# Modulation weights laid out over four column quarters, and 64-row score matmuls in the late attention

## The chip, the cores and the metric

The kernel runs on one core of a Trainium2 chip. The core has TensorE (matmuls, PE in the profile; its weight loads are the rows PEld), VectorE (DVE), ScalarE (ACT), GpSimd (POOL) and SyncE (SP, which here only issues DMAs). The metric is the device time of one launch in microseconds, lower is better. The kernel before takes 2261.13 us, the median of three runs (2259.18 to 2261.45).

## The reference, cut to what matters

Two transformer blocks over 256 tokens of width 2048, all in float32: the first with NSA attention, a feed-forward layer of 8192 and a gated embedding, the second (below) with a modulation computed from a vector `c`, a sliding-window attention (SWA), a latent attention (MLA) and another feed-forward layer.

```python
c_act = jax.nn.silu(c)                       # 1 x 2048
mod = c_act @ w_mod[l] + b_mod[l]            # w_mod: 2048 x 12288, 100.7 MB
sh1, sc1, g1, sh2, sc2, g2 = jnp.split(mod, 6, axis=-1)
h = rmsnorm(x, attn_norm_g[l]) * (1.0 + sc1) + sh1
proj = h @ w_in[l]
...
# SWA: 16 heads of width 64 over two key heads, keys of two blocks of 128
s = einsum('bnqhgd,bnkhd->bnhgqk', qb, k_band) * (64 ** -0.5) + bias, masked, with sinks
# MLA: 8 heads, scores are the sum of a 128-wide and a 64-wide (rotary) product
s = (einsum('bqhd,bkhd->bhqk', qn_i, k_nope) + einsum('bqhd,bkd->bhqk', qr_i, k_rope)) * scale
...
x = x + g1 * (mix @ w_out[l])
u = relu((rmsnorm(x, mlp_norm_g[l]) * (1.0 + sc2) + sh2) @ w_ff1[l])
x = x + g2 * ((u * u) @ w_ff2[l])
```

## The kernel before, in words

**The large products.** Each weight matrix comes in units of 1 MB (`raw`, four slots). A unit makes two steps. For each step ACT copies the rounded upper part (`split`, L498), DVE subtracts it from the raw value to get the lower part (`split`, L913), and TensorE multiplies both with the split activations `xs` or `hidden`. A group is eight steps and 512 output columns. In the form `columns` (L1528, L1533) a step is 16 matmuls, in the form `tokens` (L1517 to L1519) it is 12. `upper` and `lower` have four slots too: ACT may run at most four steps ahead of TensorE, and DVE follows ACT.

**The modulation.** `mod` belongs to the second block but does not depend on it, so its weights are read during the first. A mod unit is 128 rows of `w_mod` by the 2048 columns of one of six sections: one DMA of 1 MB into `modraw` (two slots), row r in partition r. `add_mod` (L917 to L930) multiplies the 128 rows by 128 values of silu(c), one for each partition, and adds to `modacc`, 128 x 2048, one DVE instruction a unit (L927; the first unit of a section is a plain multiplication, L925). After 16 units `sum_mod` (L1587) transposes `modacc` in 16 blocks of 128 x 128 on TensorE (L1592), and `store_mod` (L932) sums over the former partitions with two DVE reductions (L940) and adds the bias (L943). There are 96 mod units, two to a group, placed by hand: `group` of DVE calls `add_mod` behind the steps 3 and 6, SP issues the units behind the third and the fourth weight unit of a group (`group`, L320), and TensorE makes the sums of a section between two steps of a later group. In the stage of the gated embedding (`gated`, `regained`) DVE has the residual, two sums of squares and a gain to do for each group as well.

**The start.** Eleven small vectors are read as rows of 128 values into `vrow`, turned by three transposes (L1600) and copied to `vcol` (L1094, L1095). ACT and DVE form silu(c) as `silu_c`, 128 x 16: column k has the values for mod unit k.

**Late attention.** `LATE_JOBS` are four SWA jobs and two MLA jobs of four heads each. A job's scores (`score`, L1689) have a part for the first 128 queries (t=0, keys 128 wide) and one for the second (t=1, keys 256 wide). The head width of SWA and the rotary width of MLA are 64, but the matmuls run over 128 rows: a pair of heads stands in the two halves of `qa` or `qr`, and `ka` and `kr` are padded with zeros in the half of the other head. SWA adds the bias with matmuls from `toes` (L1715) behind the product of each head; MLA adds its 64-wide product behind the 128-wide one of each head. For t=1 heads 0 and 1 write one PSUM bank and heads 2 and 3 the next. DVE takes the maxima (L1230), ACT the exponentials (L707), DVE scales (L1257), TensorE transposes (L1736 to L1738) and multiplies with the values (`mix`, L1765 and L1766). In the SWA `mix` two heads write partitions 0 to 63 and 64 to 127 of one bank, with weights of 128 rows x 64 columns.

What sets the order is written out by hand for each engine; all waits are on semaphores that count.

Of the kernel before, what the change touches and what calls it, by code (L numbers as in the profile page):

```python
# [25 lines left out]
P = 128  # L26
# [26 lines left out]
MODS = 6 * KC  # L53

# [30 lines left out]
def program(nc, a):  # L85
    with ExitStack() as ctx:
# [36 lines left out]
        modacc = place("modacc", [P, D], at=M + 16384)  # L123
# [15 lines left out]
        vrow = place("vrow", [P, 3, P], at=U + 32768)  # L139
# [30 lines left out]
        vcol = place("vcol", [P, 2 * P + CMP_LEN])  # L170
        modcol = place("modcol", [P, 6, KC])
        modsum = place("modsum", [P, 2, KC // 2])
        silu_c = place("silu_c", [P, KC])
# [11 lines left out]
        COL = dict(mix=0, ffn=16, ple=32, attn=48, mlp=64, c=80, q=96, kv=99, b=P, k=P + 96, v=2 * P)  # L185
# [24 lines left out]
        rows_landed, aux_landed, consts = sem("rows_landed"), sem("aux_landed"), sem("consts")  # L210
# [73 lines left out]

        block = ctx.enter_context(nc.Block())
# [3 lines left out]
        def _(sp):  # L289
# [41 lines left out]
            for t in range(T):  # L331
                sp.dma_start(h[:, t, :], a["x"][0, t * P:(t + 1) * P, :]).then_inc(x_landed[t], 16)
            vecs = [(a["norm_mix"][0], 0, 0), (a["norm_ffn"][0], 16, 0), (a["norm_ple"][0], 32, 0),
                    (a["attn_norm_g_2"][0], 48, 0), (a["mlp_norm_g_2"][0], 64, 0), (a["c_2"][0], 80, 0),
                    (a["mla_q_norm_g_2"][0], 96, 0), (a["mla_kv_norm_g_2"][0], 99, 0),
# [5 lines left out]
            sp.dma_start(vrow[0:32, 2, :], a["nsa_cmp_pos_v"][0]).then_inc(rows_landed, 16)  # L341

# [3 lines left out]
            with loop(sp, c, 5, {lower_ready: 8, mod_added: 2}) as i:  # L346
                group(w_in, i * NW + 2 * NW, mods=section_rows(i * 2 + 4, 0))
# [16 lines left out]
            with loop(sp, c, NG - 1, {lower_ready: 8, mod_added: 2}) as i:  # L364
                group(w_out, i * NW + NW, mods=section_rows(i * 2 + 2, 1))
# [14 lines left out]
            with loop(sp, c, QUARTERS - 1, {lower_ready: 64, mod_added: 16}) as i:  # L380
# [3 lines left out]
            with loop(sp, c, NG, {lower_ready: 8, mod_added: 2}) as i:  # L384
# [23 lines left out]
        def _(pool):  # L408
# [32 lines left out]
            nc.gpsimd.memset(table[:], NEG).then_inc(bias_placed, 1)  # L441
            pool.wait_ge(bias_table, 1)
# [34 lines left out]
        def _(act):  # L477
# [164 lines left out]
            nc.scalar.activation(silu_c[:], vcol[:, COL["c"]:COL["c"] + KC], ACT.Sigmoid).then_inc(c_sigmoid, 1)  # L642
# [52 lines left out]
            def job_exps(n, kind, scale):  # L695
                for t in range(T):
# [4 lines left out]
                    for j in range(HPG):  # L701
                        w = P * (t + 1)
                        sb = banks_of(kind)[0]
                        src = ps[:, sb, P * j:P * j + P] if t == 0 else ps[:, sb + 1 + j // 2, S * (j % 2):S * (j % 2) + S]
# [192 lines left out]
        def _(dve):  # L897
# [19 lines left out]
            def add_mod(k):  # L917

                slot = st["mod"] % 2
                dve.wait_ge(mod_landed[slot], c.next(mod_landed[slot], 16))  # L920
                if st["mod"]:
                    dve.wait_ge(mod_added, c.at(mod_added))
                w, s = modraw[:, slot, :], silu_c[:, bass.ds(k, 1)]
                if isinstance(k, int) and k == 0:
                    op = nc.vector.tensor_scalar(modacc[:], w, s, None, ALU.mult)  # L925
                else:
                    op = nc.vector.scalar_tensor_tensor(modacc[:], w, s, modacc[:], ALU.mult, ALU.add)  # L927
                op.then_inc(mod_added, 1)
                c.next(mod_added)
                st["mod"] += 1  # L930

            def store_mod(m):  # L932
# [9 lines left out]
                link(op)  # L942
# [1073 lines left out]
```

## Time and profile before

| | |
|---|---|
| median of three runs | 2261.13 us |
| profiled execution, its own time | 2260.09 us |
| span of its instructions | 2258.2 us |
| granted TensorE clock over the span | 0.993 |
| PE busy | 2197.9 us (97%) |
| DVE busy | 1510.6 us (67%) |
| ACT busy | 1014.5 us (45%) |
| DMA | 499.5 MB, mean 221 GB/s |

The profile is of one execution; times inside it are counted from the first instruction. Busy time of PE is matmul time with modelled ends, so the starts of matmuls and weight loads say more than their lengths. A duration like 2347 ns of a DVE instruction is that instruction alone. In a timeline, neighbouring instructions of one kind are merged: `x8` is eight of them, from the start of the first to the end of the last, and square brackets tell how long the engine had been idle and what ended it. A float32 matmul that is not of the split kind is two passes in the profile, so a score product of one head is two rows x2. A transpose is one.

### The profile page before, as it was taken

What the parts mean: (1) busy time and instruction counts of PE and PEld (TensorE: products, weight loads), DVE (VectorE), ACT (ScalarE), POOL (GpSimd) and SP (SyncE); (2) the same over time, 40 slices, a digit from 0 to 9 for tenths busy, and PEclk for the clock granted to TensorE, in tenths of its full rate; (3) what the DMA queues carried; (4) which work ended last, traced back from release to release, by engine and by line L of the source; (5) the groups of instructions that cost most, each with busy time, mean ns of one, the idle gap of its engine ahead of it and who ended that gap; (6) DMA issues with size and microseconds to landing.
All of it is one profiled execution on the core that took longest, in us unless ns stands there. A gap on an engine that the chain in (4) does not pass through costs nothing.

```text
span 2258.2 us, 29043 instructions
## 1 busy us (share of the span) xinstructions
PE 2197.9 (97%) x11458; PEld 1879.8 (83%) x11458; DVE 1510.6 (67%) x1455; ACT 1014.5 (45%) x1263; POOL 15.2 (1%) x40
## 2 busy tenths in 40 slices
PE   7999999999999999999999899999999999999997
PEld 6888888788888888888878698887888888888886
DVE  6676566778677778777778866557655555555655
ACT  5443373544344344344354645545434444443442
POOL 1000000000000000000000000000000000000000
PEclk9999999999999999999999999999999999999999
DMA  8876407687877877877867463364566655655563
GB/s 313 302 265 196 154 19 298 240 281 277 300 259 288 294 277 257 318 271 284 294 237 278 125 199 118 134 202 149 185 195 193 192 187 186 198 188 192 186 198 118
DMA packets 213096, 499.50 MB, mean 221 GB/s; under 512 B 10068, under 2 KB 12680, under 8 KB 199800
## 3 DMA queue, kind: packets, MB, share of 16 engines
q1 hardware_dynamic: 211528, 491.16, 63.3%
q0 software_dynamic: 1456, 6.72, 0.8%
q8 instruction: 86, 1.41, 0.3%
q14 instruction: 26, 0.21, 0.0%
HBM read 495.68 MB, written 2.17 MB: 220 GB/s over the span
## 4 chain that ended last, share of the span: by engine, by line
PE 60%; issue 36%; DVE 2%; ACT 1%; DMA 1%; SPq 0%; POOL 0%; DVEq 0%; ACTq 0%; POOLq 0%
PE ps L1528 17%; PE ps L1517 9%; PE ps L1518 9%; PE ps L1519 9%; PE ps L1533 9%; PE ps L1709 2%; PE ps L1765 1%; PE ps L1628 1%; PE ps L1575 1%; PE ps L1592 0%; PE ps L1715 0%; ACT prob L707 0%; PE ps L1766 0%; PE ps L1763 0%; DMA raw<-in_nsa_w_in_dram 0%
## 5 line engine op out<-in xcount | busy, mean ns | idle before, releaser
L913 DVE TENSOR_TENSOR lower<-raw,upper 128x1024 fp32r<-128x1024 f32 (+2 forms) x733 | 883.9, 1216 | 517.1 <-ACT upper L498 513.7
L498 ACT ACTIVATE upper<-raw 128x1024 fp32r<-128x1024 f32 (+2 forms) x733 | 770.1, 1056 | 943.7 <-PE ps L1519 530.2
L1528 PE MATMUL ps<-xs,upper 128*128 128x512 f32 x2688 | 677.0, 394 | 0.6 <-DVE xs L1068 0.4
L1528 PEld LDWEIGHTS ps<-xs,upper 128*128 128x128 f32 x2688 | 485.8, 190 | 88.8 <-DVE xs L1068 0.8
L1517 PE MATMUL ps<-upper,hidden 128*128 128x512 f32 x1024 | 399.2, 390 | 0.0
L1518 PE MATMUL ps<-lower,hidden 128*128 128x512 f32 x1024 | 398.5, 389 | 0.0
L1519 PE MATMUL ps<-upper,hidden 128*128 128x512 f32 x1024 | 398.4, 389 | 0.0
L1533 PEld LDWEIGHTS ps<-xs,lower 128*128 128x128 f32 x2688 | 366.7, 190 | 26.2
L1533 PE MATMUL ps<-xs,lower 128*128 128x256 f32 x2688 | 374.8, 282 | 0.0
L1517 PEld LDWEIGHTS ps<-upper,hidden 128*128 128x128 f32 x1024 | 192.3, 188 | 40.3 <-DVE lower L913 0.9
L1519 PEld LDWEIGHTS ps<-upper,hidden 128*128 128x128 f32 x1024 | 192.3, 188 | 39.8
L1518 PEld LDWEIGHTS ps<-lower,hidden 128*128 128x128 f32 x1024 | 192.3, 188 | 39.5
L927 DVE SCALAR_TENSOR_TENSOR modacc<-modraw,silu_c,modacc 128x2048 f32<-128x2048 f32 x90 | 211.2, 2347 | 0.3
L1517 PE MATMUL ps<-upper,xs 128*128 128x512 f32 (+1 forms) x512 | 199.5, 390 | 3.1 <-DVE lower L913 1.9
L1519 PE MATMUL ps<-upper,xs 128*128 128x512 f32 (+1 forms) x512 | 196.9, 385 | 0.0
L1518 PE MATMUL ps<-lower,xs 128*128 128x512 f32 (+1 forms) x512 | 196.8, 384 | 0.0
L1517 PEld LDWEIGHTS ps<-upper,xs 128*128 128x128 f32 x512 | 96.3, 188 | 24.5 <-issue 4.1
L1519 PEld LDWEIGHTS ps<-upper,xs 128*128 128x128 f32 x512 | 96.1, 188 | 19.1
L1518 PEld LDWEIGHTS ps<-lower,xs 128*128 128x128 f32 x512 | 96.3, 188 | 17.8
L525 ACT ACTIVATE half<-ps 128x1024 f32<-128x1024 f32 x41 | 42.2, 1028 | 75.9 <-PE ps L1533 75.9
L980 DVE TENSOR_TENSOR summed<-ps,half 128x1024 f32<-128x1024 f32 x32 | 39.2, 1225 | 50.5 <-ACT half L525 50.5
L538 ACT ACTIVATE hidden<-summed 128x1024 fp32r<-128x1024 f32 x32 | 34.1, 1064 | 51.3 <-DVE summed L982 51.3
(259 smaller groups left out, 1160.1 us busy)
## 6 DMA issues: line engine op xcount, KB each, us to landing
raw<-in_ffn_w_dram SPq DMA_DIRECT2D x128, 1024.0 KB, 5.4
raw<-in_w_ff_dram SPq DMA_DIRECT2D x128, 1024.0 KB, 5.1
modraw<-in_w_mod_dram SPq DMA_DIRECT2D x96, 1024.0 KB, 7.3
raw<-in_nsa_w_in_dram SPq DMA_DIRECT2D x40, 1024.0 KB, 5.2
raw<-in_nsa_w_out_dram SPq DMA_DIRECT2D x16, 1024.0 KB, 7.3
raw<-in_ple_w_gate_dram SPq DMA_DIRECT2D x16, 1024.0 KB, 5.4
raw<-in_w_out_dram SPq DMA_DIRECT2D x16, 1024.0 KB, 5.0
raw<-in_w_in_dram SPq DMA_DIRECT2D x12, 1024.0 KB, 5.3
```

Of the source, the lines that this page charges most:

```text
L498: nc.scalar.activation(dst, src, ACT.Copy).then_inc(upper_ready, 1)
L525: nc.scalar.activation(half[:], ps[:, 4 * parity:4 * parity + 4, S:2 * S], ACT.Copy).then_inc(half_copied, 1)
L538: nc.scalar.activation(hidden[:, 4 * g:4 * g + 4, 0, :], summed[:], ACT.Copy).then_inc(hidden_upper, 1)
L913: nc.vector.tensor_tensor(low, src, up, ALU.subtract).then_inc(lower_ready, 1)
L927: op = nc.vector.scalar_tensor_tensor(modacc[:], w, s, modacc[:], ALU.mult, ALU.add)
L980: done(nc.vector.tensor_tensor(summed[:], ps[:, 4 * parity:4 * parity + 4, 0:S], half[:], ALU.add))
L1517: mm(out, xu, up[:, kk, :], start=first, stop=False)
L1518: mm(out, xu, low[:, kk, :], start=False, stop=False)
L1519: op = mm(out, xl, up[:, kk, :], start=False, stop=last)
L1528: mm(ps[:, 4 * par + f, :], up[:, kk, f * P:(f + 1) * P], both, start=(k == 0), stop=False, skip_group_check=True)
L1533: op = mm(ps[:, 4 * par + f, 0:S], low[:, kk, f * P:(f + 1) * P], x[:, k, 0, :], start=False, stop=(k == KC - 1), skip_group_check=True)
L1709: op = mm(out, q, k, start=first, stop=False, skip_group_check=True)
```

## The change

**Layout.** A mod unit is still 128 rows by 2048 columns, but partition 4b+q now holds rows b, 32+b, 64+b and 96+b, of each only the 512 columns of quarter q. It comes in four DMAs of 256 KB (`PARTS = 4`), runs of 2 KB instead of 8 KB. `modacc` is 128 x 512. A unit is added in four DVE instructions of 128 x 512, one for each m (rows 32m to 32m+31), each waiting for the one before it. After 16 units only four transposes are left, all into bank 2, and one DVE reduction of 128 x 512 with a stride of four sums over the 32 partitions of each quarter. `silu_c` becomes 128 x 64: each value of c four times side by side, which GpSimd writes as a copy with repetition (L457 of the new kernel) before a fourth transpose at the start.

**Scores.** For t=1 of the late jobs the 64-wide products run over 64 rows only, heads alternating between rows 0 to 63 and 64 to 127, and neighbouring heads write different banks (`late_place`). The products of the four heads now come first, and the bias matmuls, or MLA's 64-wide products, behind all four. For t=0 this order changes too, while the rows stay 128.

```diff
         modraw = place("modraw", [P, 2, D], at=M)
-        modacc = place("modacc", [P, D], at=M + 16384)
+        modacc = place("modacc", [P, D // PARTS], at=M + 16384)
...
+        def late_place(kind, j):
+            return (1 + j // 2, j % 2) if kind == "nsa" else (1 + j % 2, j // 2)
...
                 if st["mod"] >= 2:
-                    sp.wait_ge(mod_added, c.next(mod_added))
+                    sp.wait_ge(mod_added, c.next(mod_added, PARTS))
                 st["mod"] += 1
-                sp.dma_start(modraw[:, slot, :], w_mod[row, col]).then_inc(mod_landed[slot], 16)
+                src = w_mod[row, col].rearrange("(m b) (q n) -> b q m n", b=ROWS, q=PARTS)
+                for m in range(PARTS):
+                    sp.dma_start(modraw[:, slot, m * NW:(m + 1) * NW], src[:, :, m, :]).then_inc(mod_landed[slot], 16)
...
+            sp.dma_start(vrow[0:PARTS * KC, 3, 0:ROWS], a["c_2"][0].rearrange("(m b) -> m b", b=ROWS)).then_inc(rows_landed, 16)
...
+            pool.wait_ge(rows_landed, 16 * 11)
+            nc.gpsimd.tensor_copy(vrow[0:PARTS * KC, 4, :].rearrange("m (b q) -> m b q", q=PARTS),
+                                  vrow[0:PARTS * KC, 3, 0:ROWS].unsqueeze(2).to_broadcast([PARTS * KC, ROWS, PARTS])).then_inc(c_spread, 1)
...
-                dve.wait_ge(mod_landed[slot], c.next(mod_landed[slot], 16))
-                if st["mod"]:
-                    dve.wait_ge(mod_added, c.at(mod_added))
-                w, s = modraw[:, slot, :], silu_c[:, bass.ds(k, 1)]
-                if isinstance(k, int) and k == 0:
...
+                dve.wait_ge(mod_landed[slot], c.next(mod_landed[slot], 16 * PARTS))
+                for m in range(PARTS):
+                    if st["mod"] or m:
+                        dve.wait_ge(mod_added, c.at(mod_added))
+                    w, s = modraw[:, slot, m * NW:(m + 1) * NW], silu_c[:, bass.ds(k * PARTS + m, 1)]
+                    if isinstance(k, int) and k == 0 and m == 0:
+                        op = nc.vector.tensor_scalar(modacc[:], w, s, None, ALU.mult)
+                    else:
+                        op = nc.vector.scalar_tensor_tensor(modacc[:], w, s, modacc[:], ALU.mult, ALU.add)
...
-                for i, bank in enumerate((2, 6)):
-                    op = nc.vector.tensor_reduce(modsum[:, i], ps[:, bank:bank + 2, :].rearrange("p b (k n) -> p (b k) n", n=P),
-                                                 AX.X, ALU.add)
+                link(nc.vector.tensor_reduce(modsum[:].rearrange("p (i q) -> p i q", q=PARTS),
+                                             ps[:, 2, :].rearrange("p (i b q) -> p i q b", b=ROWS, q=PARTS), AX.X, ALU.add))
...
-                for k in range(KC):
-                    op = nc.tensor.transpose(ps[:, (2, 3, 6, 7)[k // 4], k % 4 * P:(k % 4 + 1) * P],
-                                             modacc[:, k * P:(k + 1) * P], ident[:])
+                for i in range(PARTS):
+                    op = nc.tensor.transpose(ps[:, 2, i * P:(i + 1) * P], modacc[:, i * P:(i + 1) * P], ident[:])
...
+                    for j in range(HPG):
+                        out = outs[j]
+                        first = j == 0 if t == 0 else late_place(kind, j)[1] == 0
                         hh = HPG * i + j
+                        r = slice(0, P) if t == 0 else slice(64 * (hh % 2), 64 * (hh % 2) + 64)
...
                         elif kind == "swa":
-                            pairs = [(qa[:, hh // 2, t * P:(t + 1) * P], ka[:, i // 2, hh % 2, 0:w])]
+                            op = mm(out, qa[r, hh // 2, t * P:(t + 1) * P], ka[r, i // 2, hh % 2, 0:w], start=first, stop=False,
+                                    skip_group_check=True)
...
+                        if kind == "mla":
+                            op = mm(outs[j], qr[r, hh // 2, t * P:(t + 1) * P], kr[r, hh % 2, 0:w], start=False, stop=False,
+                                    skip_group_check=True)
```

DVE in the second group of the gated embedding, in program order, before: `h<-h,gainrow` is the gain, `modacc` the two mod units, `lower` the splits of the weights.

```order
L1352 TENSOR_TENSOR h<-h,gainrow 128x2x512
L1340 ISA xn,sumsq_114<-h 128x512
L1340 ISA sumsq_114 128x1
L927 SCALAR_TENSOR_TENSOR modacc<-modraw,silu_c,modacc 128x2048
L913 TENSOR_TENSOR lower<-raw,upper 128x1024 x3
L927 SCALAR_TENSOR_TENSOR modacc<-modraw,silu_c,modacc 128x2048
L913 TENSOR_TENSOR lower<-raw,upper 128x1024 x4
```

The same place of the changed kernel, with what each instruction waits for:

```order
L1360 ISA xn,sumsq_114<-h 128x512 [waits gained]
L1360 ISA sumsq_114 128x1
L946 SCALAR_TENSOR_TENSOR modacc<-modraw,silu_c,modacc 128x512 [waits mod_added,mod_landed0,squares_v]
L946 SCALAR_TENSOR_TENSOR modacc<-modraw,silu_c,modacc 128x512 [waits mod_added] x3
L931 TENSOR_TENSOR lower<-raw,upper 128x1024 [waits upper_ready] x3
L946 SCALAR_TENSOR_TENSOR modacc<-modraw,silu_c,modacc 128x512 [waits mod_added,mod_landed1]
L946 SCALAR_TENSOR_TENSOR modacc<-modraw,silu_c,modacc 128x512 [waits mod_added] x3
L931 TENSOR_TENSOR lower<-raw,upper 128x1024 [waits upper_ready] x4
```

Nothing has changed its place; each unit has become four chained instructions.

TensorE in the first late job (SWA), t=0 and then t=1, before: `ka,qa` are the products, `flip,toes` the bias.

```order
L1709 MATMUL ps<-ka,qa 128x128
L1715 MATMUL ps<-flip,toes 128x128
L1709 MATMUL ps<-ka,qa 128x256
L1715 MATMUL ps<-flip,toes 128x128 x2
L1709 MATMUL ps<-ka,qa 128x256
L1715 MATMUL ps<-flip,toes 128x128 x2
```

The whole job in the changed kernel:

```order
L1732 MATMUL ps<-ka,qa 128x128 x4
L1746 MATMUL ps<-flip,toes 128x128 x4
L1732 MATMUL ps<-ka,qa 128x256 x4
L1746 MATMUL ps<-flip,toes 128x128 x8
L1994 MATMUL ps<-ident,qrope 128x128 x8
```

The four products of a part now follow one another, and the bias of all four heads comes behind them. The number of matmuls is the same.

## Rows read from the trace of the kernel before

**Rows 1.** The page, busy time of the engines.

```profile
PE 2197.9 (97%) x11458; PEld 1879.8 (83%) x11458; DVE 1510.6 (67%) x1455; ACT 1014.5 (45%) x1263; POOL 15.2 (1%) x40
```

**Rows 2.** Stretches: busy of PE, PEld, DVE, ACT, POOL; clock, DMA share, GB/s.

```profile
500.00:600.00 100.00, 100.00 (x491) 84.66 (x490) 74.08 (x57) 41.84 (x40) 0.00 (x0) 1.00 0.81 293
1200.00:1300.00 100.00, 89.83 (x404) 73.59 (x403) 82.93 (x96) 54.66 (x75) 0.00 (x0) 0.95 0.57 194
1800.00:1900.00 100.00, 100.00 (x462) 83.56 (x461) 58.20 (x48) 40.25 (x39) 0.00 (x0) 1.00 0.58 190
```

**Rows 3.** Waits of weight loads: us, times, longest.

```profile
PEld ps L1517 <- DVE lower L913: 2.2, 6, 0.4
```

**Rows 4.** Weight loads around the third section sum, first feed-forward.

```profile
712.35 1.90 PEld L1592 LDWEIGHTS ps<-ident,modacc 128*128 128x128 f32 x16
714.22 0.19 PEld L1517 LDWEIGHTS ps<-upper,hidden 128*128 128x128 f32 x1
719.83 0.19 PEld L1517 LDWEIGHTS ps<-upper,hidden 128*128 128x128 f32 x1 [0.28 <-DVE lower L913]
```

**Rows 5.** DVE around the same section sum.

```profile
712.06 1.23 DVE L989 TENSOR_TENSOR hidden<-summed,hidden 128x1024 fp32r<-128x1024 f32 x1
714.52 2.36 DVE L940 TENSOR_REDUCE modsum<-ps 128x8 f32<-128x1024 f32 x2 [1.24 <-PE ps L1592]
717.36 1.29 DVE L925 TENSOR_SCALAR modacc<-modraw,silu_c 128x2048 f32<-128x2048 f32 x1
718.56 3.49 DVE L913 TENSOR_TENSOR lower<-raw,upper 128x1024 fp32r<-128x1024 f32 x3
```

**Rows 6.** Groups of DVE: shape, count | us, mean ns | idle before.

```profile
L927 DVE SCALAR_TENSOR_TENSOR modacc<-modraw,silu_c,modacc 128x2048 f32<-128x2048 f32 x90 | 211.2, 2347 | 0.3
L1083 DVE SCALAR_TENSOR_TENSOR h<-h,norm,gainrow 128x1024 f32<-128x1024 f32 x4 | 4.9, 1279 | 1.1 <-DMA gainrow<-in_final_norm_g_dram 1.1
L1047 DVE TENSOR_SCALAR xn<-h,norm 128x512 f32<-128x512 f32 x20 | 8.4, 484 | 0.2
L982 DVE SCALAR_TENSOR_TENSOR summed<-summed 128x1024 f32<-128x1024 f32 x32 | 39.2, 1225 | 1.1
```

**Rows 7.** DVE in the second gated group, and the PEld row there.

```profile
1201.98 2.35 DVE L927 SCALAR_TENSOR_TENSOR modacc<-modraw,silu_c,modacc 128x2048 f32<-128x2048 f32 x1
1204.25 3.49 DVE L913 TENSOR_TENSOR lower<-raw,upper 128x1024 fp32r<-128x1024 f32 x3
1205.52 0.19 PEld L1517 LDWEIGHTS ps<-upper,xs 128*128 128x128 f32 x1 [0.45 <-DVE lower L913]
```

**Rows 8.** DVE and PE in a first feed-forward group, and at the start.

```profile
648.43 3.49 DVE L913 TENSOR_TENSOR lower<-raw,upper 128x1024 fp32r<-128x1024 f32 x3
651.24 1.09 PE L1528 MATMUL ps<-xs,upper 128*128 128x512 f32 x4
...
41.09 3.54 DVE L913 TENSOR_TENSOR lower<-raw,upper 128x1024 fp32r<-128x1024 f32 x3
44.84 1.32 PE L1528 MATMUL ps<-xs,upper 128*128 128x512 f32 x5
```

**Rows 9.** Fourth late job, t=1: a head's product, its bias; DVE's maximum.

```profile
1407.41 0.60 PE L1709 MATMUL ps<-ka,qa 128*128 128x256 f32 x2
1407.85 0.61 PE L1715 MATMUL ps<-flip,toes 128*128 128x128 f32 x4
...
1411.13 1.22 DVE L1230 TENSOR_REDUCE stat<-ps 128x4 f32<-128x1024 f32 x1 [0.58 <-PE ps L1715]
```

**Rows 10.** Weight loads around an SWA product with the values, 64-column weights.

```profile
1412.02 0.14 PEld L1738 LDWEIGHTS ps<-ident,prob 128*128 128x128 f32 x1
1412.33 0.20 PEld L1765 LDWEIGHTS ps<-probT,tok 128*64 128x64 f32 x4 [0.17 <-issue]
1412.60 0.36 PEld L1766 LDWEIGHTS ps<-probT,tok 128*64 128x64 f32 x4
1413.83 0.30 PEld L1709 LDWEIGHTS ps<-kn,qn 128*128 128x128 f32 x2 [0.17 <-issue]
```

More of the change, by code:

```diff
@@ L53 @@
 MODS = 6 * KC
+PARTS = 4
+ROWS = P // PARTS
 class Counts:
@@ L640, in _ @@
             to_features(vcol[:, COL["mix"]:COL["mix"] + KC], ahead=2)
-            nc.scalar.activation(silu_c[:], vcol[:, COL["c"]:COL["c"] + KC], ACT.Sigmoid).then_inc(c_sigmoid, 1)
+            nc.scalar.activation(silu_c[:], vcol[:, COL["c"]:COL["c"] + PARTS * KC], ACT.Sigmoid).then_inc(c_sigmoid, 1)
             group([first_half])
@@ L1696, in score @@
                         pe.wait_ge(exps, 2 * n - 1 + t)
+                    outs = []
                     for j in range(HPG):
-                        out = ps[:, sb, P * j:P * j + P] if t == 0 else ps[:, sb + 1 + j // 2, S * (j % 2):S * (j % 2) + S]
-                        first = j == 0 if t == 0 else j % 2 == 0
+                        bank, half_ = late_place(kind, j)
+                        outs.append(ps[:, sb, P * j:P * j + P] if t == 0 else ps[:, sb + bank, S * half_:S * half_ + S])
@@ L1700, in score @@
+                    for j in range(HPG):
+                        out = outs[j]
+                        first = j == 0 if t == 0 else late_place(kind, j)[1] == 0
                         hh = HPG * i + j
+                        r = slice(0, P) if t == 0 else slice(64 * (hh % 2), 64 * (hh % 2) + 64)
                         if kind == "nsa":
-                            pairs = [(heads[:, hh, t * P:(t + 1) * P], heads[:, 24 + 4 * b + i, 0:w])]
+                            op = mm(out, heads[:, hh, t * P:(t + 1) * P], heads[:, 24 + 4 * b + i, 0:w], start=first, stop=False,
+                                    skip_group_check=True)
@@ L1703, in score @@
                         elif kind == "swa":
-                            pairs = [(qa[:, hh // 2, t * P:(t + 1) * P], ka[:, i // 2, hh % 2, 0:w])]
-                        else:
-                            pairs = [(qn[:, hh, t * P:(t + 1) * P], kn[:, hh, 0:w]),
-                                     (qr[:, hh // 2, t * P:(t + 1) * P], kr[:, hh % 2, 0:w])]
-                        for q, k in pairs:
-                            op = mm(out, q, k, start=first, stop=False, skip_group_check=True)
-                            first = False
+                            op = mm(out, qa[r, hh // 2, t * P:(t + 1) * P], ka[r, i // 2, hh % 2, 0:w], start=first, stop=False,
+                                    skip_group_check=True)
+                        else:
+                            op = mm(out, qn[:, hh, t * P:(t + 1) * P], kn[:, hh, 0:w], start=first, stop=False,
+                                    skip_group_check=True)
@@ L1711, in score @@
+                    for j in range(HPG):
+                        hh = HPG * i + j
+                        r = slice(0, P) if t == 0 else slice(64 * (hh % 2), 64 * (hh % 2) + 64)
+                        if kind == "mla":
+                            op = mm(outs[j], qr[r, hh // 2, t * P:(t + 1) * P], kr[r, hh % 2, 0:w], start=False, stop=False,
+                                    skip_group_check=True)
                         if kind == "swa":
@@ L1880, in _ @@
             group_turned(tokens, 3)
-            group(tokens, xs, n=320, between={1: lambda: sum_mod(6 * KC), 4: turn_modulation})
+            group(tokens, xs, n=320, between={1: lambda: sum_mod(6 * PARTS * KC), 4: turn_modulation})
             group(columns, xs, between={4: turn_latents})
```

74 lines of the change are left out of this document (41 added, 33 removed).

## The prediction

> **What bounds the kernel now.** I read first the busy time of the engines [rows 1]: TensorE is busy for 97% of the span, DVE for 67%. A share is a mean, so next the stretches [rows 2]: in the first feed-forward, where modulation units are read and added, TensorE is busy for 100.00 of 100 us, DVE for 74, and the DMA engines for 0.81. In the second feed-forward, without those units, TensorE is again at 100.00. Only the stretch 1200 to 1300 has holes (PE 89.83), and there DVE is busy for 82.93. Then the waits [rows 3]: weight loads of the token groups waited for DVE's `lower` six times, 2.2 us in all. So the kernel is TensorE's almost everywhere: what is taken from its queue comes off the time one to one, what DVE gets in addition costs nothing while it stays within its lead, and the lead is gone at those six places.
>
> **The change, part by part.** The sum is made against the profiled execution, 2260.09 us (span 2258.2 and 1.9 around it); the median of the runs, 2261.13, is 1.0 above it.
>
> *Section sums, removed from TensorE.* Sixteen transposes last from 712.35 to the next group's load at 714.22, 1.87 us or 0.117 each [rows 4]. Four remain. Twelve fewer are 1.40 us, and six sections make 8.4 us. Is what follows then late? In the feed-forward DVE is at the sum at 713.29 (712.06 + 1.23) and waits 1.24 us for the transposes [rows 5]; with the transposes 1.40 earlier it starts at 713.3, 1.2 earlier. Its two reductions of 2.36 us become one of half a bank pair's width: `TENSOR_REDUCE` of 128x1024 takes 1.22 [rows 9], less 512 elements at 0.534 (the step between 1279 and 2347 ns for 1024 elements, halved [rows 6]) gives 0.69, so 1.67 us less. Behind it stands the first unit of the next section, which now has one plain multiplication and three multiply-adds. The distance to the next split was 1.20 (717.36 to 718.56) [rows 5] and becomes 0.48 for the first [rows 6] and 0.745 for each of the three (1279 ns for 128x1024 less 534 [rows 6]), with gaps of 0.03 between them (1.1 us over 32 at L982, which waits for its own predecessor [rows 6]), less the overlap of 0.08 with the next: 2.73, so 1.53 more. Net the split comes 1.2 + 1.67 - 1.53 = 1.34 us earlier, and TensorE wants it 1.40 earlier. The stall of 0.28 that stands there [rows 4] stays as it is within 0.1. I count nothing for it, and the whole 8.4 for the transposes.
>
> *The additions, lengthened on DVE.* A unit took 2.27 us of DVE's time (1201.98 to 1204.25) [rows 7]. Four of 0.745 with three gaps of 0.03, less the same 0.08, are 2.99, so 0.72 more. The elements are the same; it is three more fixed parts of about 0.21 and three waits on the own result. The trace has no multiply-add of this form at 128x512, so both ends: with the fixed part of L982 (1225 ns for 1024 elements, less 1068, is 0.16 [rows 6]) it is 0.47, and if each wait cost 0.25 more than I think it is 1.5. I take 0.72, the nearest form. Where does it show?
> - In the gated embedding the first of three splits behind the unit ends at 1204.25 + 1.22 = 1205.47, and TensorE, idle for it, starts at 1205.52 [rows 7]. No lead is left, so the 0.72 goes straight into TensorE. DVE's chain there begins anew with each group's residual, so it is paid in each of the three groups whose first unit stands behind `regained`: 2.2 us (1.4 to 4.5).
> - In the first feed-forward the corresponding split ends at 649.65 and TensorE needs it at 651.24 [rows 8]: 1.6 us of lead, 0.9 left. There are twelve such groups. Nothing, but this cover is thin: beyond a growth of 1.5 each of them would pay.
> - At the start two units stand one behind the other, 1.53 + 0.72 = 2.25 later. The split behind them ends at 41.09 + 1.22 = 42.31, and TensorE needs it at 44.84 [rows 8]: 2.5 of lead, so 0.25 left. Nothing, up to 0.3.
>
> *Four DMAs for one.* On SP's queue 288 more issues. A unit's four stand in front of the next weight unit, but SP spends most of its time waiting for free slots, and a weight unit has three others ahead of it. The DMA engines: two of six megabytes a group change from runs of 8 KB to 2 KB. The weights have runs of 2 KB already, and where only they move, 190 GB/s takes a share of 0.58, that is 328 GB/s if full [rows 2]. At that rate the 293 GB/s of the modulated stretch would take 0.89 instead of 0.81. Under 1, so nothing. The start also gets a copy on GpSimd and a fourth transpose in front of `vcol`; DVE reaches that point only after scaling its tile, and TensorE then waits for a weight unit's split on ACT. Nothing, up to 0.3 us.
>
> *Late scores.* For t=1 a head's product is two passes of 256 columns: the bias starts 0.44 us after the product (1407.41, 1407.85) [rows 9]. So the four products of a job take eight passes, 1.74 us. In pairs over different rows two passes would run side by side. Row pairs do not occur in this trace, but column pairs do: the SWA product with the values issues four loads in 0.20 us and its 256-wide passes get to the next form 0.27 us after the first (1412.33, 1412.60) [rows 10], although in program order the two forms alternate by head. So passes of two heads do overlap there. At that rate four pairs take 0.87, and 0.87 is saved. MLA's 64-wide products are the same. What goes against it are the borders of the stretch: the last full-width load before the column pairs starts at 1412.02, the next would be due at 1412.13 at the pace of transposes and starts at 1412.33, and the first behind them has 0.17 of idle again [rows 10]. I take 0.15 for each border, 0.30 a job. Net 0.57, six jobs (four SWA, two MLA): 3.4 us. Ends: 5.2 gained without borders, 1.8 lost if pairs do not overlap. Can the gain be used? DVE's maximum over t=1 waited 0.58 us for these matmuls [rows 9], so in SWA just the 0.57 goes through, and more would not.
>
> The page TensorEngine Tiling of the Trainium skill says under Key Properties that changing the tiling mode drains the engine, while different tiles may load and multiply in parallel. This speaks against short tiled stretches like these. The idle 0.17 us at both borders agrees with it; by the second half of the rule alone the late scores would give 5.2, by both 3.4.
>
> **Sum.** -8.4 + 2.2 - 3.4 = -9.6: 2250.5 against the profiled execution, and 1.0 more, 2251.5 us, against the median.
>
> **Rivals.**
> - *Row pairs don't run side by side.* Then the scores only gain two borders a job: -8.4 + 2.2 + 1.8 = -4.4, 2256.7 us. For it: no row of this trace shows two row halves at once, and both write all 128 partitions, of different banks. Against it: column pairs overlap [rows 10]. Chance 0.10.
> - *The chained additions cost more,* 1.5 us a unit. The gated embedding loses 4.5 instead of 2.2, the start 1.3 (1.53 + 0.78 + 1.5 = 3.8 against 2.5 of lead), the twelve feed-forward groups nearly nothing: -8.4 + 4.5 + 1.3 - 3.4 = -6.0, 2255.1 us. For it: a wait on the own result in front of every instruction, and indices from registers in the loops. Against it: such waits cost 0.03 at L982. Chance 0.08.
> - *The DMA engines become the bound, slower than before.* Weights take 195 of the 293 GB/s, a share of 0.595 at 328 GB/s, so the modulation's 98 GB/s took 0.215, at 456 GB/s. The place is the modulated stretch, some 1000 us; it decides once the share passes 1, with the modulation at 98 / 0.405 = 242 GB/s, and the kernel is slower than before below about 236, where 1% of 1000 us eats the gain. At 230 GB/s the share is 1.02 and the time 2251.5 + 21 = 2272. For it: four small DMAs, each with its own completion, of which the trace has no stream. Against it: the weights' 328 GB/s with the same runs. Chance 0.04.
>
> The page DMA: Bandwidth & Descriptors of the Trainium skill, under its measured HBM to SBUF table, advises batches of 1 MiB or more; 256 KB would stand far below that. It is the last rival's mechanism. No run so far shows 256 KB DMAs in a row, so it is not excluded.
>
> **How the numbers follow.** The forecast has 0.78. Its own range is 2249 to 2254. The lower end of what the bounds allow is -8.4 + 1.4 - 5.2 = -12.2, 2248.9; towards the other side the second and first rivals end at 2255.1 and 2256.7. The range 2248.5 to 2257 leaves out the DMA rival and the tails. A change of 0.2%, 4.5 us, is about what a measurement of this kernel can tell from none; the border is 2256.6. Faster: nearly all of the forecast, most of the second rival, half of the first, 0.84. The same: 0.12. Slower: 0.04.
>
> **What would show it.** Four transposes and about 0.5 us at each section sum. DVE's multiply-adds of 128x512 at about 745 ns, and a unit in 3.0 us. PE's waits for `lower` in the three gated groups near 1.1 us each, and none in the feed-forward groups. The DMA share of the feed-forward below 0.9. Late products with 64-row weights starting in pairs, four products in about 0.9 us, a job 0.5 to 0.6 shorter. It is wrong if those products start one by one, if `lower` is waited for in the feed-forward, or if ACT waits for weights there.

## The result, and the profile after

The changed kernel takes 2251.55 us (median of 6, 2250.84 to 2253.38); the kernel before, on the same chip, 2260.86 us (median of 6, 2259.18 to 2261.92). The ratio is 0.9961, 95% interval 0.9951 to 0.9971. The forecast was 2251.5. The profiled execution took 2251.8 us, span 2249.9, at a mean granted clock of 0.991.

The page after, with the lines that answer to [rows 1] and the first of [rows 6]; the last line is the modulation's DMAs (count, KB each, us from issue to landing):

```profile
PE 2187.3 (97%) x11387; PEld 1867.7 (83%) x11387; DVE 1563.6 (69%) x1737; ACT 1013.3 (45%) x1263; POOL 15.4 (1%) x41
L946 DVE SCALAR_TENSOR_TENSOR modacc<-modraw,silu_c,modacc 128x512 f32<-128x512 f32 x378 | 283.7, 751 | 15.3 <-DVE modacc L946 1.7
modraw<-in_w_mod_dram SPq DMA_DIRECT2D x384, 256.0 KB, 5.4
```

DVE has 53 us more to do and TensorE 11 less, and the kernel is faster, because DVE's additional work lies beside TensorE's nearly everywhere. The stretches that answer to [rows 2], with the same columns:

```profile
500.00:600.00 100.00, 100.00 (x481) 84.29 (x480) 80.71 (x85) 42.18 (x41) 0.00 (x0) 1.00 0.84 298
1190.00:1290.00 100.00, 87.57 (x386) 71.41 (x385) 87.14 (x114) 53.62 (x74) 0.00 (x0) 0.93 0.55 189
1800.00:1900.00 100.00, 100.00 (x464) 83.66 (x463) 57.26 (x48) 40.11 (x38) 0.00 (x0) 1.00 0.59 193
```

In the feed-forward DVE went from 74 to 81 of 100 us, TensorE stayed at 100.00. The DMA share went from 0.81 to 0.84. Of the three, only the gated stretch lost busy time. The waits that answer to [rows 3]:

```profile
PEld ps L1537 <- DVE lower L931: 4.1, 6, 1.2
```

The third section sum, weight loads first, then DVE, for [rows 4, 5]:

```profile
709.16 0.58 PEld L1612 LDWEIGHTS ps<-ident,modacc 128*128 128x128 f32 x4
709.71 0.19 PEld L1537 LDWEIGHTS ps<-upper,hidden 128*128 128x128 f32 x1
715.22 0.19 PEld L1537 LDWEIGHTS ps<-upper,hidden 128*128 128x128 f32 x1 [0.19 <-DVE lower L931]
```

```profile
708.87 1.23 DVE L1008 TENSOR_TENSOR hidden<-summed,hidden 128x1024 fp32r<-128x1024 f32 x1
710.02 0.69 DVE L958 TENSOR_REDUCE modsum<-ps 128x16 f32<-128x512 f32 x1
711.00 0.19 DVE L961 TENSOR_TENSOR modcol<-modsum,vcol 128x16 f32 x1 [0.29 <-DVE modsum L958]
711.19 0.49 DVE L944 TENSOR_SCALAR modacc<-modraw,silu_c 128x512 f32<-128x512 f32 x1
711.71 2.33 DVE L946 SCALAR_TENSOR_TENSOR modacc<-modraw,silu_c,modacc 128x512 f32<-128x512 f32 x3
713.95 3.49 DVE L931 TENSOR_TENSOR lower<-raw,upper 128x1024 fp32r<-128x1024 f32 x3
```

From the first transpose to the next load it is 0.55 us now (709.16 to 709.71) and was 1.87. DVE no longer waits for the transposes. The second gated group, DVE and the load that waits, for [rows 7]:

```profile
1196.09 3.12 DVE L946 SCALAR_TENSOR_TENSOR modacc<-modraw,silu_c,modacc 128x512 f32<-128x512 f32 x4
1199.12 3.49 DVE L931 TENSOR_TENSOR lower<-raw,upper 128x1024 fp32r<-128x1024 f32 x3
1200.39 0.19 PEld L1537 LDWEIGHTS ps<-upper,xs 128*128 128x128 f32 x1 [1.21 <-DVE lower L931]
```

A unit lasts 3.03 us (1196.09 to 1199.12) for 2.27, and the load's wait grew from 0.45 to 1.21. The leads of [rows 8], in a first feed-forward group and at the start:

```profile
646.00 3.49 DVE L931 TENSOR_TENSOR lower<-raw,upper 128x1024 fp32r<-128x1024 f32 x3
648.05 2.00 PE L1548 MATMUL ps<-xs,upper 128*128 128x512 f32 x8
...
42.79 3.49 DVE L931 TENSOR_TENSOR lower<-raw,upper 128x1024 fp32r<-128x1024 f32 x3
44.13 2.04 PE L1548 MATMUL ps<-xs,upper 128*128 128x512 f32 x8
```

The split ends at 646.00 + 1.22 = 647.22 and is wanted at 648.05: 0.8 of lead, for 1.6. At the start 0.1 is left.

**Where the time went.** I paired the start of each of TensorE's 733 weight steps in the two traces and noted where the distance changes. The last step comes 8.1 us earlier:

| place | change of the distance, us |
|---|---|
| six section sums, 1.31 or 1.32 each | -7.9 |
| groups right behind four of them, 0.10 to 0.18 each | -0.5 |
| three gated groups, 0.76, 0.76, 0.77 | +2.3 |
| late attention | -3.3 |
| TensorE's clock: -1.0 near 21, +1.6 near 1166, +0.8 near 1272, -0.5 near 1537 | +0.8 |
| the start (+0.3) and many shifts below 0.1 | +0.5 |

The sums, the gated groups and the late attention are as forecast. The 0.5 behind the sums was forecast at nothing, and the clock's line is the surprise.

### The profile page after: what moved, and what is told of

Same layout as the page of the kernel before. It is cut to its first block, busy times and chain, and to the rows that moved or that the text cites. A ratio compares the mean times of both kernels' runs of the same rounds, so it can differ in the third digit from the quotient of the medians.

```text
span 2249.9 us, 29971 instructions
## 1 busy us (share of the span) xinstructions
PE 2187.3 (97%) x11387; PEld 1867.7 (83%) x11387; DVE 1563.6 (69%) x1737; ACT 1013.3 (45%) x1263; POOL 15.4 (1%) x41
## 4 chain that ended last, share of the span: by engine, by line
PE 58%; issue 37%; DVE 3%; ACT 1%; DMA 1%; SPq 0%; POOL 0%; DVEq 0%; ACTq 0%; POOLq 0%
PE ps L1548 17%; PE ps L1537 9%; PE ps L1553 9%; PE ps L1539 9%; PE ps L1538 9%; PE ps L1729 1%; PE ps L1796 1%; PE ps L1650 1%; PE ps L1595 1%; DVE lower L931 0%; DVE modacc L946 0%; PE ps L1746 0%; ACT prob L725 0%; PE ps L1797 0%; PE ps L1794 0%
## 5 line engine op out<-in xcount | busy, mean ns | idle before, releaser
L946 DVE SCALAR_TENSOR_TENSOR modacc<-modraw,silu_c,modacc 128x512 f32<-128x512 f32 x378 | 283.7, 751 | 15.3 <-DVE modacc L946 1.7
```

## The experiments

Times are medians, ratios are to the kernel before on the same chip. The changed kernel is 2251.55 above and 2252.08 in its second set of runs, on the chip that also ran mod_only, late_only and gated_later.

**The changed kernel once more.** No edit.

> The changed kernel itself once more. Theory A (terms add up: section sums -8.4 us, gated embedding +2.3, late scores -3.3, start +0.3; what else the first profile shows is TensorE's granted clock, which fell at other places than before: +1.6 near 1165, +0.8 near 1272, -1.0 near 21, -0.5 near 1537, together +0.8) expects 2251.5 us within 1, and in a second profile the same stalls, while the stretches at the lower clock differ from those of the first profile. Rival B: the change itself moves the clock's dips; then the matmuls near 1164 to 1167 and 1271 run at half clock in this profile too.

Measured 2252.08 us, ratio 0.9961 (0.9947 to 0.9974). The table's lines repeat: six sums at -1.30 to -1.32, gated 0.76, 0.76, 0.77, late -3.30. TensorE's matmuls go over to the clock's upper level at 22.1 us (20.2 in the first profile, 22.1 before), and the clock is at its lower level near 436, 1265 and 1530 in all three profiles; what moves is its edges: 1264.6 to 1274.8 us before, 1259.3 to 1272.9 in the first profile, 1261.1 to 1271.4 here. So theory A holds for these places. The fall near 1166, which before does not have, is here too, +1.61 us; for this place alone rival B is left.

**The modulation's part alone.** The changed kernel with `score`, its places and its readers as before.

```
-                            op = mm(out, qa[r, hh // 2, t * P:(t + 1) * P], ka[r, i // 2, hh % 2, 0:w], start=first, stop=False,
-                                    skip_group_check=True)
+                            pairs = [(qa[:, hh // 2, t * P:(t + 1) * P], ka[:, i // 2, hh % 2, 0:w])]
...
```

> The modulation's part alone, late scores as before. Theory A: -8.4 + 2.3 + 0.3 = -5.8 us, 2255.1 (ratio 0.9974). Rival: the profile's total of -8.3 is mostly late scores and the section sums give less, because DVE's longer unit stands behind each sum: then no better than 2257.5. In the profile: DVE waits of TensorE of 1.2 us in three gated groups, late attention as before.

Measured 2255.53 us, ratio 0.9977 (0.9968 to 0.9986): -5.1 for -5.8. Sums and gated groups shift as in the table, late attention by nothing.

**The late scores' part alone.** The pieces of the diff that concern the scores, on the kernel before.

```
+                        r = slice(0, P) if t == 0 else slice(64 * (hh % 2), 64 * (hh % 2) + 64)
...
+                            op = mm(out, qa[r, hh // 2, t * P:(t + 1) * P], ka[r, i // 2, hh % 2, 0:w], start=first, stop=False,
+                                    skip_group_check=True)
```

> The late scores' part alone, modulation as before. Theory A (64-row products over different row halves run side by side, less two borders a job): -3.3 us, 2257.6 (ratio 0.9985). Rival 1 (no overlap, only borders): +1.8 or more, 2262.7. Rival 2 (overlap, but DVE's maximum and the exponentials cap it): -1.5, 2259.4.

Measured 2256.82 us, ratio 0.9985 (0.9975 to 0.9994): -3.8; in its trace late attention is 3.29 shorter. The two parts add up: -5.1 and -3.8 make -8.9, the whole change -8.6 beside them. No fall of the clock near 1170.

**All late products over 128 rows, in the new order.**

```
-                        r = slice(0, P) if t == 0 else slice(64 * (hh % 2), 64 * (hh % 2) + 64)
+                        r = slice(0, P)
```

> The changed kernel with its new order of the late scores (the four products first, then MLA's rotated ones or the biases) but all products over 128 rows, as before the change. Theory A (the gain is the two halves side by side): the whole 3.3 us are gone, 2255.1. Rival: a part of the gain is the new order, since the maximum waits for the last product only: 2253.

Measured 2255.2 us, ratio 0.9978 (0.9968 to 0.9988); its trace is 3.27 longer in late attention than the changed kernel's. So all of the gain is the products over 64 rows, none the order.

**The halves in turn.** Heads 0, 2, 1, 3 for 0, 1, 2, 3.

```
-                    for j in range(HPG):
+                    for j in (0, 2, 1, 3) if t == 1 else range(HPG):
```

> The changed kernel with the late 64-row products in the order of heads 0, 2, 1, 3, so that the two of one row half stand behind each other. Theory A (a product overlaps with its neighbour in the queue if that uses the other half, in program order): heads 2 and 1 still overlap, the others don't, four products take 1.3 us for 0.87: +0.43 in six jobs, +2.6, 2254.4. Rival 1: the engine takes either half's next product whatever the order: no change. Rival 2: overlap needs exact alternation: +5.2, 2257.

Measured 2252.39 us, ratio 0.9964 (0.9951 to 0.9978), and late attention without a shift: my theory A was wrong, rival 1 holds. Loads around the four products of the first late job, t=1, in the changed kernel, with the halves in turn, and over 128 rows:

```profile
1379.12 0.41 PEld L1746 LDWEIGHTS ps<-flip,toes 128*128 128x128 f32 x3
1379.65 0.73 PEld L1732 LDWEIGHTS ps<-ka,qa 64*128 64x128 f32 x8
1380.71 0.19 PEld L1746 LDWEIGHTS ps<-flip,toes 128*128 128x128 f32 x1 [0.33 <-issue]
```

```profile
1380.12 0.53 PEld L1746 LDWEIGHTS ps<-flip,toes 128*128 128x128 f32 x4
1380.77 0.74 PEld L1732 LDWEIGHTS ps<-ka,qa 64*128 64x128 f32 x8
1381.84 0.19 PEld L1746 LDWEIGHTS ps<-flip,toes 128*128 128x128 f32 x1 [0.33 <-issue]
```

```profile
1378.44 0.42 PEld L1746 LDWEIGHTS ps<-flip,toes 128*128 128x128 f32 x3
1378.78 1.60 PEld L1732 LDWEIGHTS ps<-ka,qa 128*128 128x128 f32 x8
1380.40 0.19 PEld L1746 LDWEIGHTS ps<-flip,toes 128*128 128x128 f32 x1
```

Eight loads in 0.73 or 0.74 us over halves, in 1.60 over 128 rows. Inside the group of the changed kernel the loads start in pairs, 1379.651 and 1379.657, then 1379.759 and 1379.766; with the halves in turn they still do, 14 ns apart. So it costs nothing when two products of one half stand behind each other. The rows don't say which half a load is for. That a pair is one load of each half is concluded from two things. A pair starts every 0.22 us, the pace of a single pass over 128 rows, so two passes share the time of one. And in [rows 10] four loads of L1765 stand in front of four of L1766, though the program has two and two for each head, so there a head's product on one column half overtook the other head's. A run with all four heads in one row half, which would settle it, is missing. The price is at the edges: the first half load stands 0.31 us after the last full one (0.11 between full ones), and the first full one is idle for 0.33, 0.52 after the last half one (0.22 between half ones).

**The gated groups' first unit one step later.**

```
-                group([gated(g - 1), regained(g - 1)], mods=8 + 2 * g)
+                group([gated(g - 1), regained(g - 1)], mods=8 + 2 * g, at=(4, 6))
```

> The changed kernel with the first modulation unit of the three gated groups one step later (behind the split of step 4, not in front of it). Theory A: the stall of 1.16 us at step 4 goes in each of three groups, the split of step 5 keeps a lead of about 0.5, so -3.5 us against the changed kernel, 2248.0 (ratio 0.9943). Rival 1: the stall only moves to step 5 or 7, gain under 1 us, 2251. Rival 2: the later release of the modulation's buffer delays weights, since one queue issues both, and ACT waits for them: no gain or a loss.

Measured 2249.67 us, ratio 0.9949 (0.9935 to 0.9962). DVE in the second gated group:

```profile
1195.91 1.23 DVE L931 TENSOR_TENSOR lower<-raw,upper 128x1024 fp32r<-128x1024 f32 x1
1197.05 3.11 DVE L946 SCALAR_TENSOR_TENSOR modacc<-modraw,silu_c,modacc 128x512 f32<-128x512 f32 x4
1200.08 2.35 DVE L931 TENSOR_TENSOR lower<-raw,upper 128x1024 fp32r<-128x1024 f32 x2
```

The split of step 4 now stands in front of the unit, and the last lead, of step 5, is 0.47 us. In the paired steps three groups are 1.17 us shorter each, less 0.09: 3.3 of the 3.5 of theory A. The median gained 2.4 against the changed kernel's second set of runs (1.9 against the first); single executions of one kernel differ by a us or two.

**The same behind each section sum.** As above, and `at=(3, 6) if g else (4, 6)` in the second half of `quarter`.

> The run with the gated groups' units one step later, and the same in the group behind each section sum. Theory A: the stall of 0.05 to 0.15 at five sums goes too, -0.5 us against that run, 2249.2; against the changed kernel -3.9 in the profile's steps. Rival: step 5 of those groups stalls in its place: no further gain.

Measured 2248.51 us, ratio 0.9945 (0.9932 to 0.9959). Against gated_later the steps behind three sums come 0.15, 0.11 and 0.12 earlier, and at two of them the next step gives 0.10 back: 0.2 lasting, nearer to the rival than to the 0.5. The lower median is no evidence for more. The weight loads' waits for `lower` are gone from the list.

**One DMA for a unit.** The additions read the same places of the buffer, so the modulation's values are others than the reference's.

```
-                for m in range(PARTS):
-                    sp.dma_start(modraw[:, slot, m * NW:(m + 1) * NW], src[:, :, m, :]).then_inc(...)
+                sp.dma_start(modraw[:, slot, :], w_mod[row, col]).then_inc(mod_landed[slot], 16)
...
```

> The changed kernel, but each modulation unit comes by one DMA of 1 MiB with runs of 8 KB, as before the change; additions, transposes and sums as in the change, so the modulation's values are not the reference's. Theory A: the four DMAs cost nothing, 2251.8 within 0.5, while the mean time to landing and the packets fall. Rival 1: the 288 issues on the queue and the smaller runs cost, then 1 us or more faster. Rival 2, on the clock: the fall of TensorE's clock near 1165, which all four profiles with the modulation's part have and the two without it don't, comes from the DMAs' traffic; then it is absent here and 1.6 us are gained.

Measured 2251.63 us, ratio 0.9958 (0.9944 to 0.9971): no difference. Its DMA line, and the stretch 560 to 660 of it and then of the changed kernel:

```profile
modraw<-in_w_mod_dram SPq DMA_DIRECT2D x96, 1024.0 KB, 7.2
...
560.00:660.00 100.00, 100.00 (x502) 85.12 (x501) 76.00 (x78) 40.83 (x39) 0.00 (x0) 1.00 0.80 286
```

```profile
560.00:660.00 100.00, 100.00 (x502) 85.15 (x501) 76.30 (x79) 40.52 (x39) 0.00 (x0) 1.00 0.81 286
```

The same 286 GB/s take 0.80 and 0.81. The fall of the clock near 1165 is still there, so it does not need the small DMAs.

**Two parts, and eight.** `PARTS = 2` or `8`, and the widths that hang on it.

```
-PARTS = 4
+PARTS = 2            (8)
+MW = D // PARTS
...
-                    w, s = modraw[:, slot, m * NW:(m + 1) * NW], silu_c[:, bass.ds(k * PARTS + m, 1)]
+                    w, s = modraw[:, slot, m * MW:(m + 1) * MW], silu_c[:, bass.ds(k * PARTS + m, 1)]
...
```

> The changed kernel with two parts for four: partition 2b+q, units of two additions of 128x1024, sums of eight transposes. Theory A: a unit takes 2.5 us for 3.03 (two of 1.28), so the three gated stalls of 1.16 become about 0.65 (-1.5 us); four more transposes of 0.11 in six sections are +2.6. Sum +1.1 against the changed kernel: 2253. Rival: the cost of four parts lies elsewhere too (issues on the DMA queue, start), then two parts are equal or faster, 2251 or below.

Measured 2252.2 us, ratio 0.9963 (0.9949 to 0.9977). Its second gated group:

```profile
1196.17 2.61 DVE L947 SCALAR_TENSOR_TENSOR modacc<-modraw,silu_c,modacc 128x1024 f32<-128x1024 f32 x2
...
1199.97 0.19 PEld L1538 LDWEIGHTS ps<-upper,xs 128*128 128x128 f32 x1 [0.70 <-DVE lower L932]
```

The unit is 2.53 us, each gated group 0.51 shorter, each sum 0.44 longer: the +1.1 of theory A, term by term. Since the clock's fall near 1165 is absent from its profile, -1.6, the two profiles don't show a loss either, and the medians come out alike (2252.2, and 2251.55 or 2252.08).

> The changed kernel with eight parts: partition 8b+q, units of eight additions of 128x256, sums of two transposes. Theory A: 751 ns less 256 elements at 1.03 is 487, a unit 8 x (0.487 + 0.04) = 4.2 us, 1.15 more than now. Transposes -1.3; three gated groups +3.5; twelve first feed-forward groups have 0.75 of lead and pay 0.4 each, +4.8; the four groups behind a section sum have none, +4.6; the start +2.3. Sum +14, 2265.5, slower than before. Rival: the leads stretch, because the splits before them run ahead, and only the gated groups pay: +2 to +3, 2254.

Measured 2271.83 us, ratio 1.0052 (1.0039 to 1.0066), slower than before: +20 for the forecast +14. Three executions took 2270.06 to 2271.83 us, two 2276.40 and 2277.24, and the profile is of the longest. ACT near 370, then the page's group of the additions, ACT's wait for those weights, and the stretch 500 to 600:

```profile
365.13 2.00 ACT L516 ACTIVATE upper<-raw 128x1024 fp32r<-128x1024 f32 x2 [9.27 <-DMA raw<-in_nsa_w_out_dram]
382.12 2.01 ACT L516 ACTIVATE upper<-raw 128x1024 fp32r<-128x1024 f32 x2 [6.70 <-DMA raw<-in_nsa_w_out_dram]
```

```profile
L947 DVE SCALAR_TENSOR_TENSOR modacc<-modraw,silu_c,modacc 128x256 f32<-128x256 f32 x762 | 369.2, 484 | 46.4 <-DMA modraw<-in_w_mod_dram 12.8
ACT upper L516 <- DMA raw<-in_nsa_w_out_dram: 36.0, 9, 9.3
500.00:600.00 100.00, 99.58 (x491) 83.88 (x491) 90.02 (x127) 42.35 (x41) 0.00 (x0) 1.00 0.91 289
```

Its profiled execution, 25.4 us longer in span than the changed kernel's, divides so by the paired steps: start 2.7, the w_out stretch from 340 to 440 about 9.6, the feed-forward 8.5, gated groups and the rest the remaining 4.6. The start, the feed-forward and the gated part are near what theory A has (2.3; 4.8 + 4.6 less the transposes; 3.5); the w_out stretch is what it missed. There TensorE waits 2.4 and 3.8 us for weights that land late, pays 1.7 for a fall of the clock behind the second wait, and 1.3 by the clock at the norm near 436. Two things stand before the late weights. First the queue: SP's issues at the beginning of the stretch, and then a stretch of each kernel, eight_parts first:

```profile
348.86 10.22 SPq L327 DMA_DIRECT2D modraw<-in_w_mod_dram  x16
359.45 2.27 SPq L318 DMA_DIRECT2D raw<-in_nsa_w_out_dram  x3
...
375.00:380.00 5.00, 4.00 (x18) 3.00 (x16) 2.52 (x6) 0.42 (x1) 0.00 (x0) 1.00 1.10 285
```

```profile
375.00:380.00 5.00, 5.00 (x24) 4.14 (x23) 4.49 (x5) 1.69 (x3) 0.00 (x0) 1.00 1.05 387
```

Issuing one such DMA takes SP 0.54 us in the median, up to 0.60 mostly (0.35 for one of 1 MB in one_dma and before), so the sixteen of two units hold the queue for 10.2 us before the first weight unit goes out; the changed kernel's eight take 5.1. Second the engines: with 128 KB DMAs and runs of 1 KB they are full (1.10) at 285 GB/s, where the changed kernel moves 387 at 1.05. How the wait divides between the two is not shown. The changed kernel has 40.00 of 40 us busy from 345 to 385.

**Twelve idle transposes at each sum.** TensorE's work as before the change.

```
+                for k in range(12):
+                    nc.tensor.transpose(ps[:, (3, 6, 7)[k // 4], k % 4 * P:(k % 4 + 1) * P], modacc[:, 0:P], ident[:])
```

> The changed kernel with twelve idle transposes, of which nobody reads the result, ahead of the four of each section sum: TensorE's work as before the change, DVE's and the DMAs' as after. Theory A (the sums' term is only TensorE's 72 transposes): +72 x 0.11 = +7.9 us against the changed kernel, 2259.7 with the clock's fall near 1165 and 2258.1 without. On that fall: if the place of TensorE's idle time in the run decides it, TensorE stands here where it stood before the change, and the fall is absent; if DVE's or the DMAs' activity decides, it is there as in all six profiles with four parts. Rival to A: DVE, with its shorter reduction, now waits for the transposes and delays the next splits: +10 or more.

Measured 2259.02 us, ratio 0.9992 (0.9983 to 1.0001): the sums' term is TensorE's 72 transposes, 1.31 at each of six places, +7.9. And in this profile the clock does not fall near 1172; the section on the prediction comes back to why. Three microseconds from where TensorE works again after that norm (at 1163.19, 1170.50 and 1170.67), in the changed kernel, the padded one and the kernel before; the number behind the last engine's is the clock:

```profile
1163.00:1166.00 3.00, 2.81 (x8) 2.28 (x9) 2.82 (x6) 3.00 (x6) 0.00 (x0) 0.62 0.00 0
```

```profile
1170.30:1173.30 3.00, 2.80 (x12) 2.31 (x13) 2.82 (x6) 3.00 (x6) 0.00 (x0) 1.00 0.00 0
```

```profile
1170.50:1173.50 3.00, 2.83 (x13) 2.33 (x14) 2.82 (x6) 3.00 (x6) 0.00 (x0) 1.00 0.00 0
```

TensorE's idle pieces in front of it are the same in all three (1.24 or 1.25, 1.32 and 1.92 us). In the changed kernel's profile the clock then goes down to its lower level (1.2 GHz) for a part of the stretch, 0.62 in the mean, and 8 matmuls stand where the others have 12 and 13.

**The clock held.** units_later, with transposes of the identity in TensorE's gaps at four norms.

```
+                before, between = {1: (30, 0), 2: (10, 14), 3: (80, 0), 4: (40, 0)}.get(norms, (0, 0))
+                for _ in range(before):
+                    nc.tensor.transpose(ps[:, b0 + 3, 0:P], ident[:], ident[:])
...
+                for _ in range(between):
+                    nc.tensor.transpose(ps[:, 4 * p + 3, 0:P], ident[:], ident[:])
```

> The same with idle transposes in TensorE's gaps at four norms (30 near 430, 10 and 14 near 1160, 80 near 1258, 40 near 1520), into banks that nobody reads. Theory A (the clock falls for lack of work and can be held by any work): no stretch at the lower clock but the one near 20; gains 1.6 near 1165, 1.5 near 1270, 0.8 near 436, 0.5 near 1530, together -4.4 against units_later, 2244.8. Rival 1: transposes of 128 columns don't hold the clock: no gain. Rival 2: they run past the end of the gaps and cost what they gain: 2249.

Measured 2246.65 us, ratio 0.9936 (0.9923 to 0.9950), the best of the study; 1.9 below units_later, not 4.4. The stretch that answers to 1163 to 1166 above, and then TensorE's gap at the third of these norms in units_later and here:

```profile
1163.00:1166.00 3.00, 2.89 (x13) 2.35 (x14) 2.85 (x6) 3.00 (x6) 0.00 (x0) 1.00 0.00 0
```

```profile
1262.00:1266.00 4.00, 0.68 (x4) 0.71 (x5) 3.08 (x11) 2.54 (x6) 0.00 (x0) 0.50 0.00 0
```

```profile
1262.00:1266.00 4.00, 1.96 (x17) 1.75 (x17) 3.90 (x9) 3.54 (x8) 0.00 (x0) 1.00 0.13 20
```

Near 1165 the 1.56 us came back, near 436 1.46. Near 1264 the clock was held and gave 0.1: TensorE waits there for DVE, at either clock. Near 1525 it fell all the same, later, and cost 0.9. So two of four places paid.

## Why the prediction was right, and what it missed

- *Section sums, -8.4.* Measured -8.4, of two pieces that were each a little off: a transpose is 0.109 us of TensorE's time, not 0.117, so the sums give 7.9; and the stall behind them, forecast unchanged within 0.1, shrank by 0.10 to 0.18 at four sums. sums_padded confirms the first piece alone.
- *Additions, +2.2.* Measured +2.3 in the trace: a unit at 3.03 us for 2.99, instructions of 751 ns for 745. eight_parts shows that the thin leads were real: 1.2 us more a unit, and the feed-forward pays.
- *Leads.* The feed-forward has 0.8 left for 0.9, the start 0.1 for 0.25; no wait appeared there.
- *DMAs, nothing.* Confirmed by one_dma. The DMA share is 0.84, where I had estimated 0.89: four 256 KB DMAs with runs of 2 KB cost the engines 0.01 more than one of 1 MiB. The rival of DMA engines as the bound falls for four parts. In eight_parts it is real (a share of 1.10 at 285 GB/s), in the w_out stretch rather than the feed-forward, and together with a price that the prediction counted as nothing and that is nothing up to four parts: 0.54 us of SP's queue for each issue.
- *Late scores, -3.4.* Measured -3.3. The overlap saves 0.87 a job as forecast (1.60 less 0.73). The edges are dearer than my 0.30: 0.20 going in and 0.30 coming out; but the biases behind start quicker, 1.78 us for sixteen against 1.89, so the net in the first job is 0.46, and over all six 0.55 on average against 0.57. From the start of one job to that of the next the gains are 0.47, 0.01, 1.23, 0.47, 0.55 and 0.56; why the second and third share so unevenly is open. DVE's maximum over t=1, which waited 0.49 to 0.58 us for TensorE in the SWA jobs 2 to 4, no longer waits in them.
- *The rivals* of separate starts and of dear chaining fall by the 0.73 above and by the gap of 0.04 in front of an addition (15.3 us over 378).
- *Missed:* the granted clock. In nine profiles of kernels with shorter sums (all those with four parts but sums_padded and clock_held, and eight_parts) it fell near 1165, at 1185 in eight_parts, the same place of the program, and cost 1.6 us; in none of before, late_only, two_parts and sums_padded. DVE's and the DMAs' work is the same in sums_padded and in the changed kernel, so what runs beside TensorE does not decide. Nor does the moment counted from the kernel's start: after_again and two_parts come to this place within 0.1 us of each other, and only the first has the fall. The clock's records in the traces say more. Within one execution all changes of the clock keep to one regular beat, and the place of this beat against the program differs between executions. In the nine profiles the next beat came 0.24 to 1.46 us after TensorE's return from the third idle piece, and there the clock fell; in the other four it came 1.75 to 2.37 us after, and the clock stayed (after_again 0.84, two_parts 2.00). So the fall goes with where the beat stood, and whether the change has a hand in it is open. This was read from thirteen profiles afterwards, and no run was made to test it. The page TensorE: Matmul & The Clock Gate of the Trainium skill (Part 1) says that the chip's watch over TensorE runs on by itself and is not set anew when a kernel starts; the beats that stand elsewhere in each execution agree with it.
- *Luck in the number.* The forecast terms came to -9.6 and measured -9.4, the 0.5 behind the sums included. The clock (+0.8) and small shifts (+0.5), for which the prediction has no term, leave 8.1 in the profiles; the medians of six differ by 9.3. That the clock's line is only +0.8 is chance: near 1166 and 1272 it cost 2.4, and near 21 and 1537 it gave back 1.5. So a match within 0.05 us says nothing beyond a match within one or two.

## What to carry to other kernels

An engine that is busy for 74% of a stretch took 7 points more at no cost there, because each instruction that the bound engine waits for still ended before it was wanted; read that lead step by step, since it was gone in three gated groups and behind the section sums, and down to 0.8 us in twelve groups. Where it is gone, look first at the order: the unit moved behind the next split gave back 3.3 us in the trace, more than the growth had cost. Short products over 64 rows of different halves overlap whatever their order, and each such stretch costs about 0.5 us at its edges, so of the 0.87 that four products over 256 columns save, about 0.5 is kept.

## What the runs showed of the hardware that was not expected

- Products over 64 rows of different halves run two at a time even where two of one half stand behind each other in the program: pairs start 14 ns apart for 6, with no loss (2252.39 against 2252.08 us). The two halves behave as if each had a queue of its own, which is concluded and not seen directly.
- DVE's multiply-add of fp32 takes 2347, 1282, 751 and 484 ns for 2048, 1024, 512 and 256 columns: about 1.04 ns a column and 0.22 us fixed, and 0.04 for the wait on its own predecessor.
- Four DMAs of 256 KB land in 5.4 us each, one of 1 MiB in 7.2, at the same 286 GB/s in the stretch 560 to 660. Issuing one takes SP 0.54 us in the median for 256 as for 128 KB, and 0.35 for 1 MiB in one piece with runs of 8 KB.
- With 10 to 80 idle transposes in a gap the granted clock stays at its upper level (2.4 GHz, 1.00 in the stretches 1163 to 1166 and 1262 to 1266), where it fell without them. Near 1525, with 40 of them, it fell all the same.
